# One block for both products of each MLP, and one two-column product for the sums of squares behind them

## The chip, the cores and the metric

One Trainium2 chip, one of its cores. The metric is device time in microseconds (us) of one execution of the whole kernel. The kernel before takes 2442.57 us, the median of three runs (2442.16 to 2447.31).

## The reference

The kernel computes two transformer layers and a third with a mixer and experts, for 512 tokens of 1024 features, in 32-bit floats. The change touches the MLP of the first two layers and the norm behind each:

```python
D_MODEL, SEQ, D_FF, NORM_EPS = 1024, 512, 4096, 1e-6

def rms_norm(x, g):
    xf = x.astype(jnp.float32)
    y = xf * lax.rsqrt(jnp.mean(xf * xf, axis=-1, keepdims=True) + NORM_EPS)
    return (y * g.astype(jnp.float32)).astype(x.dtype)

def modulate(h, shift, scale):
    return h * (1 + scale) + shift

def squared_relu_mlp(h, w1, w2):
    return jnp.square(jax.nn.relu(h @ w1)) @ w2

# in each of the first two layers
h = modulate(rms_norm(x, mlp_norm[layer]), sh_m, sc_m)
x = x + gt_m * squared_relu_mlp(h, mlp_w1[layer], mlp_w2[layer])
# behind the second layer: the final norm, and then the norm of the mixer of what it gives
x = rms_norm(x, final_norm)
```

Behind the first MLP one norm of x follows. Behind the second two norms follow each other (`final_norm`, then the mixer's), so two sums are needed for each token: of x squared, and of (x times the gain of `final_norm`) squared.

## The kernel before

Features lie on the partitions and tokens along the rows. `xT` is the residual stream (8 tiles of 128 features by 512 tokens), `hT` the normed input, `hid` (in `big`) the 32 tiles of hidden features, `ring` four slots of 2 MB for weights from memory. Every phase is a `Phase` with its own semaphores and a `Block`, in which each engine gets its instructions in the order written; at the end of a block all engines meet at a barrier, and GpSimd then clears the phase's semaphores one by one. No scheduler is at work: a semaphore wait in the text is a wait on the engine.

`phase_mlp` (line 862) is called twice, for "mlp1_a"/"mlp2_a" (here MLP A) and "mlp1_b"/"mlp2_b" (MLP B, with `inner`, the gain of `final_norm`). In both it holds two phases:

- Block 1, h @ w1. After a first chunk done plainly (L954) come 14 `pairs` with Winograd's form of Strassen's method: seven products `P1` to `P7` (L940) instead of eight, whose inputs are sums made on VectorE (L1037 to L1043) and whose results VectorE adds up (L1066 to L1083). ScalarE copies `P1` (L1019) and applies relu and square (L1002, L1004). Between these VectorE multiplies weights of the next conditioning vector (L890, `ada`), and adds their bias at the end (L1088).
- Block 2, hid @ w2. 32 `steps` in two halves of output features; each step has the seven products of two matmuls (L1148), with sums made by VectorE in `sums` (L1236 to L1251) one step ahead and one L890 per step. `outputs` (L1272 to L1292, `joined` L1258) adds a half into `xT`. ScalarE squares tiles of `xT` (L379; with the gain, L381). VectorE adds the squares of the first half's four tiles together (L390). TensorE sums squares over the features in `token_sums` (L1177): each of the four 128-token parts of a tile is loaded as weights and multiplied by a column of ones.

The tail of block 2 sets the end of the phase. On TensorE it is: `token_sums` of the accumulated first half (once for `sq1`, in MLP B again for `sq2`), four `keep_busy` products (L416) whose result nobody reads, `token_sums` of tiles j = 4 to 7 (in MLP B twice each), three `keep_busy`, and `spread_rows` (L407) with the inverse root. The buffers of squares alternate, so ScalarE waits for `token_sums` of j = 4 before it squares j = 6, and of j = 5 before j = 7. In MLP B VectorE makes the last two of the `sq2` squares (L1318).

```python
                for j in range(4, 8):
                    pe.wait_ge(sqd, j + 1)
                    token_sums(m.ps[:, 1, 0:NT], sq1.at(j), False, j == 7).then_inc(summed, 1)
                    if inner is not None:
                        pe.wait_ge(sqd2, j + 1)
                        token_sums(m.ps[:, 2, 0:NT], sq2.at(j), False, j == 7).then_inc(summed2, 1)
```

`prefetch` issues the loads of both streams from the sync engine's queue, each when its ring slot is free; weight chunks are released by TensorE, conditioning chunks by VectorE, in turn. In the experts, later, weights are loaded as fast as the memory gives them. The line numbers in the rows are those of the kernel before.

Of the kernel before, what the change touches and what calls it, by code (L numbers as in the profile page):

```python
# [21 lines left out]
ACT = mybir.ActivationFunctionType  # L22
# [839 lines left out]
def phase_mlp(nc, m, name1, name2, shift, gate, cvec, mod_out, mod_bias, width, gains, inner=None):  # L862
# [48 lines left out]

    with Phase(nc) as ph:
# [5 lines left out]
            "c22", "flat"))  # L918
        outs = [(shift, m.hT)]
        with nc.Block(no_gpsimd_drain=True) as block:  # L920
# [10 lines left out]
            @block.sync  # L931
            def _(sp):
                prefetch(m, sp, name1)

# [62 lines left out]

            @block.scalar
            def _(act):
                def squared(f, h, n):  # L1000
                    part = hid[:, f, h * H:(h + 1) * H]
                    act.activation(part, part, ACT.Relu).then_inc(flat, 1)  # L1002
                    act.wait_ge(flat, n)
                    act.activation(part, part, ACT.Square)  # L1004
# [4 lines left out]
                for j in range(4):  # L1009
                    act.wait_ge(mm, j + 1)  # L1010
                    act.activation(hid[:, j, :], m.ps[:, j, :], ACT.Relu).then_inc(relu, 1)  # L1011
                    act.wait_ge(relu, j + 1)
                    act.activation(hid[:, j, :], hid[:, j, :], ACT.Square)
                for i, (c, q) in enumerate(pairs):
# [12 lines left out]
                    squared(f, 1, 4 * i + 4)  # L1027

            @block.vector
            def _(dve):  # L1030
# [29 lines left out]
                for i, (c, q) in enumerate(pairs):  # L1060
# [29 lines left out]
    at2, n2 = STREAM[name2]  # L1090
    sq1, sq2 = Squares(m, 0), Squares(m, 3)
    steps = [(half, c, k) for half in range(2) for c in range(4) for k in range(4)]
    order = [4 * half + j for half in range(2) for j in (2, 3, 0, 1)]
    flat_h = m.hT[:].rearrange("p k t -> p (k t)")
    v1, v2, v3, v4 = oflat[:, 3072:3584], oflat[:, 3584:4096], flat_h[:, 3072:3584], flat_h[:, 3584:4096]
    cres = m.rs[:]
    inner2 = m.tmp[:, 1024:1032]

    def chunk2(half, c):
        return (at2 + 2 * (4 * half + c)) % RING, 16 * ((at2 + 2 * (4 * half + c)) // RING + 1)  # L1100

    def weight_quarters(half, c, k):
        w = m.ring[:, chunk2(half, c)[0], :].rearrange("p (k n) -> p k n", k=8)
        return w[:, k, 0:256], w[:, 4 + k, 0:256], w[:, k, 256:512], w[:, 4 + k, 256:512]

    def row_quarters(c, k):
        return hid[:, 8 * c + k, 0:H], hid[:, 8 * c + k, H:T], hid[:, 8 * c + 4 + k, 0:H], hid[:, 8 * c + 4 + k, H:T]

    def sums_of(s):
        return [oflat[:, 1536 * (s % 2) + 256 * j:1536 * (s % 2) + 256 * (j + 1)] for j in range(6)]  # L1110

    with Phase(nc) as ph:
        sem = ph.sem
        added, mod_done, chn, sqd, freed, sqd2, freed2, summed, whole, rooted, inverse = (
            sem(s) for s in ("added", "mod_done", "chn", "sqd", "freed", "sqd2",
                             "freed2", "summed", "whole", "rooted", "inverse"))
        summed2 = sem("summed2")
        prod, st12_ok, st3_ok, st4_ok, p1_ok, u2_ok, u4_ok, u3_ok, c22_ok, c11_ok, c21_ok, c12_ok, scaled = (
            sem(s) for s in ("prod", "st12_ok", "st3_ok", "st4_ok", "p1_ok", "u2_ok", "u4_ok", "u3_ok", "c22_ok", "c11_ok",
                             "c21_ok", "c12_ok", "scaled"))  # L1120
        with nc.Block(no_gpsimd_drain=True) as block:
            @block.sync
            def _(sp):
                prefetch(m, sp, name2)

            @block.tensor
            def _(pe):
                def products(s, names):
                    half, c, k = steps[s]
                    first, final = c == 0 and k == 0, c == 3 and k == 3  # L1130
                    a11, a12, a21, a22 = weight_quarters(half, c, k)
                    b11, b12, b21, b22 = row_quarters(c, k)
                    s1, s2, s4, t1, t2, t4 = sums_of(s)
                    of = dict(P1=(a11, b11), P2=(a12, b21), P3=(s4, b22), P4=(a22, t4), P5=(s1, t1), P6=(s2, t2), P7=(a21, b12))
                    for name in names:
                        if name == "P6":
                            pe.wait_ge(st12_ok, s + 1)
                        if name == "P7":
                            pe.wait_ge(st3_ok, s + 1)
                        if name == "P4":  # L1140
                            pe.wait_ge(st4_ok, s + 1)
                        if first and half:
                            for taken in dict(P1=[p1_ok], P6=[u2_ok], P5=[u4_ok, c22_ok], P7=[u3_ok], P2=[c11_ok], P4=[c21_ok],
                                              P3=[c12_ok])[name]:
                                pe.wait_ge(taken, 1)
                        a, b = of[name]
                        for q in range(2):
                            ins = pe.matmul(m.ps[:, bank[name], q * H:(q + 1) * H], a[:, q * P:(q + 1) * P], b,  # L1148
                                            start=(first and q == 0), stop=(final and q == 1))
                        ins.then_inc(prod, 1)  # L1150

                def released(chunk):


                    pe.wait_ge(prod, PRODUCTS * 4 * (chunk + 1))
                    pe.sem_inc(m.free[chunk2(chunk // 4, chunk % 4)[0]], 1)

                pe.wait_ge(m.full[chunk2(0, 0)[0]], chunk2(0, 0)[1])
                for s in (0, 1):
                    products(s, ["P1", "P2"])  # L1160
                for s in (0, 1):
                    products(s, ["P6", "P5", "P7", "P4", "P3"])
                for s in range(2, len(steps) - 2):
                    half, c, k = steps[s]
                    if k == 0:
                        pe.wait_ge(m.full[chunk2(half, c)[0]], chunk2(half, c)[1])
                    products(s, ["P1"])
                    if k == 0:
                        released(s // 4 - 1)
                    products(s, ["P6", "P5", "P7", "P2", "P4", "P3"])  # L1170
                for name in ("P1", "P6", "P5", "P7", "P2", "P4", "P3"):
                    for s in (len(steps) - 2, len(steps) - 1):
                        products(s, [name])

                def token_sums(out, sq, start, stop):
                    for i in range(NT):
# [24 lines left out]
            def _(act):  # L1201
                for half in range(2):
                    act.wait_ge(prod, PRODUCTS * 30 + 2 if half else PRODUCTS * 15 + 1)
                    if half:
                        act.wait_ge(c21_ok, 1)
# [2263 lines left out]
```

## Time and profile before

| what | value |
| --- | --- |
| median of 3 runs | 2442.57 us |
| the profiled execution, its own time | 2444.82 us |
| its span (first to last instruction) | 2443.0 us |
| TensorE busy | 2305.6 us, 94% |
| VectorE busy | 1125.5 us, 46% |
| ScalarE busy | 504.7 us, 21% |
| GpSimd busy | 43.0 us, 2% |
| mean of memory traffic | 189 GB/s |

Busy time is a share of the whole span, over stages with different limits; what a part of the kernel is worth is read from the timeline at its place. An instruction of TensorE in the program shows as two in the records of these 32-bit products (x16 is eight instructions). Idle time before a group stands in brackets with what ended it; "PEq" and a line is the sequencer of TensorE at that line, at the end of a block the barrier.

### The profile page before, as it was taken

How to read it: one execution, taken by the hardware profiler on the slowest of the kernel's cores; microseconds unless marked ns; L12 is line 12 of the kernel's file. 1: busy time of each engine (PE TensorE's matmuls, PEld its weight loads, DVE VectorE, ACT ScalarE, POOL GpSimd, SP SyncE). 2: the span in 40 equal slices, each digit the busy share in tenths (PEclk: the TensorE clock that was granted, in tenths of full speed). 3: DMA queues.
4: the chain of work that ended last, by engine and by line, in shares of the span. 5: the costliest groups of instructions: out<-in, count | busy, mean ns of one | idle time of the engine just before them, and what ended most of it. 6: DMA issues, size and time to landing. Idle time of an engine off the chain costs nothing. (4 is left out here: it accounts for less than half of the span.)

```text
span 2443.0 us, 25463 instructions
## 1 busy us (share of the span) xinstructions
PE 2305.6 (94%) x9476; PEld 1461.8 (60%) x9476; DVE 1125.5 (46%) x2602; ACT 504.7 (21%) x1140; POOL 43.0 (2%) x50
## 2 busy tenths in 40 slices
PE   7999899999999999989999999999999998889886
PEld 4444457888887655554688888854555443333332
DVE  4444435666776256661455667667524211111004
ACT  2233212330002144440333100112223000000001
POOL 0000000000000000000000000000000000000000
PEclk8999999999999899989999999999999999999999
DMA  7544213353532211102453435311032679999995
GB/s 302 219 175 165 103 69 138 143 202 138 206 139 112 62 59 52 61 35 103 175 204 144 201 142 203 138 69 69 1 138 104 253 309 427 427 426 426 423 424 223
DMA packets 45453, 452.65 MB, mean 185 GB/s; under 512 B 7784, under 2 KB 7784, under 8 KB 20240
## 3 DMA queue, kind: packets, MB, share of 16 engines
q1 hardware_dynamic: 37616, 435.64, 44.7%
q0 software_dynamic: 6528, 12.17, 1.4%
q10 hardware_dynamic: 1184, 3.19, 0.3%
q8 instruction: 77, 1.26, 0.2%
q14 instruction: 48, 0.39, 0.0%
HBM read 444.54 MB, written 18.39 MB: 189 GB/s over the span
## 5 line engine op out<-in xcount | busy, mean ns | idle before, releaser
L2857 PE MATMUL ps<-ring,big 128*64 128x512 f32 (+1 forms) x768 | 232.2, 609 | 27.9 <-issue 15.7
L1148 PE MATMUL ps<-big,ring 128*128 128x256 f32 x768 | 187.4, 382 | 4.4 <-PEq L920 4.4
L2857 PEld LDWEIGHTS ps<-ring,big 128*64 128x64 f32 (+1 forms) x768 | 85.0, 150 | 146.0 <-issue 132.8
L1148 PEld LDWEIGHTS ps<-big,ring 128*128 128x128 f32 x768 | 146.9, 192 | 25.4 <-issue 5.2
L537 PE MATMUL ps<-hT,ring 128*128 128x512 f32 x336 | 153.6, 607 | 5.6 <-DMA ring<-in_stream 5.6
L940 PE MATMUL ps<-hT,ring 128*128 128x256 f32 x672 | 154.3, 379 | 1.5 <-ACT big L1011 1.5
L2953 DVE TENSOR_TENSOR big<-big,ps 128x512 f32<-128x512 f32 x20 | 13.7, 687 | 294.4 <-ACT big L2922 280.3
L1938 PE MATMUL ps<-hT,ring 128*128 128x512 f32 x320 | 143.9, 605 | 2.7 <-DVE big L2320 1.7
L940 PEld LDWEIGHTS ps<-hT,ring 128*128 128x128 f32 x672 | 127.5, 190 | 20.3 <-issue 3.1
L890 DVE SCALAR_TENSOR_TENSOR ring<-ring,tmp 128x1024 f32<-128x1024 f32 x112 | 135.9, 1217 | 0.0
L2857 PE MATMUL ps<-big 128*64 128x512 f32 (+1 forms) x352 | 128.9, 600 | 7.1 <-ACT big L2918 3.3
L1148 PE MATMUL ps<-oT 128*128 128x256 f32 x512 | 120.8, 379 | 2.1 <-DVE oT L1247 2.1
L537 PEld LDWEIGHTS ps<-hT,ring 128*128 128x128 f32 x336 | 62.4, 192 | 84.2 <-issue 76.9
L814 PE MATMUL ps<-oT,ring 128*128 128x512 f32 x256 | 110.8, 593 | 1.4 <-PEq L1508 1.0
L1148 PEld LDWEIGHTS ps<-oT 128*128 128x128 f32 x512 | 97.1, 190 | 16.0 <-DVE oT L1247 2.9
L1938 PEld LDWEIGHTS ps<-hT,ring 128*128 128x128 f32 x320 | 60.8, 194 | 76.3 <-issue 74.4
L940 PE MATMUL ps<-oT 128*128 128x256 f32 x448 | 101.3, 379 | 0.0
L2857 PE MATMUL ps<-oT,big 128*64 128x512 f32 (+1 forms) x192 | 88.1, 614 | 7.7 <-issue 3.9
L2857 PE MATMUL ps<-hT,big 128*64 128x512 f32 (+1 forms) x192 | 88.2, 614 | 6.7 <-issue 3.7
L940 PEld LDWEIGHTS ps<-oT 128*128 128x128 f32 x448 | 85.1, 190 | 11.6
L1002 ACT ACTIVATE big<-big 128x256 f32<-128x256 f32 x112 | 46.7, 417 | 219.4 <-DVE big L1073 159.8
L814 PEld LDWEIGHTS ps<-oT,ring 128*128 128x128 f32 x256 | 48.3, 190 | 64.0 <-issue 64.0
(486 smaller groups left out, 3416.0 us busy)
## 6 DMA issues: line engine op xcount, KB each, us to landing
ring<-in_stream SPq DMA_DIRECT2D x99, 2048.0 KB, 8.5
ring<-in_gate SPq DMA_DIRECT2D x17, 2048.0 KB, 29.7
ring<-in_up SPq DMA_DIRECT2D x16, 2048.0 KB, 25.8
ring<-in_down SPq DMA_DIRECT2D x15, 2048.0 KB, 28.6
big<-in_up SPq DMA_DIRECT2D x9, 2048.0 KB, 25.1
big<-in_down SPq DMA_DIRECT2D x8, 2048.0 KB, 27.8
big<-in_gate SPq DMA_DIRECT2D x7, 2048.0 KB, 25.9
hT<-in_down SPq DMA_DIRECT2D x5, 2048.0 KB, 26.9
```

Of the source, the lines that this page charges most:

```text
L537: last = pe.matmul(m.ps[:, 2 + j, :], w[:, k, j * P:(j + 1) * P], m.hT[:, k, :], start=(k == 0), stop=(k == KT - 1))
L814: last = pe.matmul(m.ps[:, 4 * c + j, :], w[:, k, j * P:(j + 1) * P], actT[:, k, :], start=(k == 0), stop=(k == KT - 1))
L890: dve.scalar_tensor_tensor(w, w, 1.0, crow, ALU.mult, ALU.mult, accum_out=mod_out[:, o + j:o + j + 1]).then_inc(done, 1)
L940: ins = pe.matmul(out, a[:, k, :], b[:, k, :], start=(k == 0), stop=(k == 3))
L1002: act.activation(part, part, ACT.Relu).then_inc(flat, 1)
L1148: ins = pe.matmul(m.ps[:, bank[name], q * H:(q + 1) * H], a[:, q * P:(q + 1) * P], b, start=(first and q == 0), stop=(final and q == 1))
L1938: last = pe.matmul(m.ps[:, tile_bank(n), :], w[:, k, j * P:(j + 1) * P], m.hT[:, k, :], start=(k == 0), stop=(k == KT - 1))
L2857: ins = pe.matmul(out[a:z, :], left[:, k * P + a:k * P + z], bufs[i % WBUF][:, k * width + c * 512:k * width + (c + 1) * 512], start=(k == ...
L2953: dve.tensor_tensor(hid[:, s, :], hid[:, s, :], m.ps[:, 3 + 2 * s, :], ALU.mult).then_inc(hid_ok, 1)
```

## The change

In both MLPs the two phases become one: their semaphores are all taken at the start, `prefetch(m, sp, name2)` stands behind `prefetch(m, sp, name1)` on the sync engine, and each engine's instructions of block 2 follow those of block 1 without a barrier. What the barrier had held apart is now held by semaphores (`prod`, `p1_ok`, `c11` and the like at 14, `squared_ok` for the hidden tiles). The last `ada` of block 1 goes behind the first `sums` of block 2, and both bias additions become one at the end. The sums of squares go to PSUM bank 7 as pairs of columns; the moving operand has two columns. The accumulated first half is summed within step 24 of 32. In MLP B the second column carries the factor gain squared, so j = 4 to 7 need no scaled squares of their own. VectorE prepares these factors behind block 1.

```diff
             def _(sp):
                 prefetch(m, sp, name1)
+                prefetch(m, sp, name2)
...
+                def token_sums(sq, factor, start, stop):
+                    for i in range(NT):
+                        ins = pe.matmul(m.ps[:, 7, 2 * i:2 * i + 2], sq[:, i * P:(i + 1) * P], factor,
+                                        start=(start and i == 0), stop=(stop and i == NT - 1))
+                    return ins
...
+                        if first and not half:
+                            for taken in dict(P1=[p1_ok], P6=[u2_ok], P5=[u4_ok, c22], P7=[u3_ok], P2=[c11], P4=[c21],
+                                              P3=[c12])[name]:
+                                pe.wait_ge(taken, len(pairs))
...
                 pe.wait_ge(m.full[chunk2(0, 0)[0]], chunk2(0, 0)[1])
+                pe.wait_ge(squared_ok, squares_of(0))
...
                     products(s, ["P6", "P5", "P7", "P2", "P4", "P3"])
+                    if s == 24:
+                        pe.wait_ge(freed, 3)
+                        if inner is None:
+                            token_sums(sq1.acc, m.ones[:, 0:2], True, False)
+                        else:
+                            pe.wait_ge(freed2, 3)
+                            pe.wait_ge(weighed, 1)
+                            token_sums(sq1.acc, either[:, 0, :], True, False)
+                            token_sums(sq2.acc, either[:, 1, :], False, False)
...
-                pe.wait_ge(u4_ok, 2)
-                pe.wait_ge(freed, 3)
-                token_sums(m.ps[:, 1, 0:NT], sq1.acc, True, False)
-                if inner is not None:
-                    pe.wait_ge(c22_ok, 2)
-                    pe.wait_ge(freed2, 3)
-                    token_sums(m.ps[:, 2, 0:NT], sq2.acc, True, False)
                 released(7)
-                keep_busy(m, pe, 7, 4)
+                pe.wait_ge(v1_ok, 2)
+                keep_busy(m, pe, 0, 4)
                 for j in range(4, 8):
                     pe.wait_ge(sqd, j + 1)
-                    token_sums(m.ps[:, 1, 0:NT], sq1.at(j), False, j == 7).then_inc(summed, 1)
-                    if inner is not None:
-                        pe.wait_ge(sqd2, j + 1)
-                        token_sums(m.ps[:, 2, 0:NT], sq2.at(j), False, j == 7).then_inc(summed2, 1)
-                keep_busy(m, pe, 7, 3)
+                    token_sums(sq1.at(j), m.ones[:, 0:2] if inner is None else factors[:, order[j], :], False, j == 7
+                               ).then_inc(summed, 1)
+                keep_busy(m, pe, 0, 3)
...
-                        if inner is not None and j < 6:
+                        if inner is not None and j < 4:
                             square_rows(m, act, sq2, inner, j, freed2, sqd2, order[j])
...
                     if i + 1 < len(pairs):
                         sums_b(*pairs[i + 1], i + 1)
-                    ada(c, 2 * q + 1, 2 * q + 2)
-                dve.wait_ge(mod_done, 8 * tiles)
-                dve.tensor_tensor(mod_out[:, 0:8 * tiles], mod_out[:, 0:8 * tiles], mod_bias[:, 0:8 * tiles], ALU.add)
+                        ada(c, 2 * q + 1, 2 * q + 2)
...
                 if inner is not None:
-                    c1.link(dve.tensor_tensor(inner2, inner, inner, ALU.mult))
+                    dve.wait_ge(c11, len(pairs))
+                    c2.link(dve.memset(factors[:, :, 0], 1.0))
+                    c2.link(dve.memset(either, 0.0))
+                    for j in range(2):
+                        c2.link(dve.memset(either[:, j, j:j + 1], 1.0))
+                    dve.tensor_tensor(factors[:, :, 1], inner, inner, ALU.mult).then_inc(weighed, 1)
                 sums(0)
+                ada(7, 3, 4)
...
                 outputs(1)
-                if inner is not None:
-                    for j in (6, 7):
-                        f = order[j]
-                        dve.wait_ge(summed2, j - 5)
-                        dve.scalar_tensor_tensor(sq2.at(j), m.xT[:, f, :], inner2[:, f:f + 1], m.xT[:, f, :], ALU.mult, ALU.mult
-                                                 ).then_inc(sqd2, 1)
```

Where the blocks of MLP A meet, on VectorE: first the rows before (L1083 is the last addition of block 1, L1088 the bias addition, L1236 to L1251 are `sums(0)`), then those of the change.

```order
L1083 TENSOR_TENSOR big<-tmp,ps 128x256 [waits u4_ok,prod]
L890 SCALAR_TENSOR_TENSOR ring,mod<-ring,tmp 128x1024
L1088 TENSOR_TENSOR mod<-mod,vec 128x32 [waits mod_done]
L920 UNCONDITIONAL_BRANCH
L1223 UNCONDITIONAL_BRANCH [waits barrier_Pool_Activation_PE_DVE_SP_release]
L1236 TENSOR_TENSOR oT<-ring 128x256 [waits full2]
L1237 TENSOR_TENSOR oT<-oT,ring 128x256 [waits chn]
L1240 TENSOR_TENSOR oT<-big 128x256
L1241 TENSOR_TENSOR oT<-big,oT 128x256 [waits chn]
```

```order
L1223 TENSOR_TENSOR big<-tmp,ps 128x256 [waits u4_ok,prod]
L1242 TENSOR_TENSOR oT<-ring 128x256 [waits prod,squared_ok,full2]
L1243 TENSOR_TENSOR oT<-oT,ring 128x256 [waits chn2]
L1246 TENSOR_TENSOR oT<-big 128x256
L1247 TENSOR_TENSOR oT<-big,oT 128x256 [waits chn2]
L1248 TENSOR_TENSOR ring<-ring 128x256
L1250 TENSOR_TENSOR big<-big 128x256
L1256 TENSOR_TENSOR oT<-ring,oT 128x256 [waits st12_ok]
L1257 TENSOR_TENSOR oT<-big,oT 128x256 [waits chn2]
L890 SCALAR_TENSOR_TENSOR ring,mod<-ring,tmp 128x1024
```

The barrier and the bias addition are gone from between the blocks, the first sums follow the last addition directly, and the L890 stands behind them.

The tail of MLP B on TensorE, before and then with the change (L1177 and L1040 are `token_sums`, L416 `keep_busy`, L407 `spread_rows`):

```order
L1148 MATMUL ps<-big,oT 128x256 x4
L1177 MATMUL ps<-ones,hT 128x1 x8
L416 MATMUL ps<-con 128x128 x4
L1177 MATMUL ps<-ones,hT 128x1 x32
L416 MATMUL ps<-con 128x128 x3
L407 MATMUL ps<-con,st 128x128 x4
```

```order
L1068 MATMUL ps<-big,oT 128x256 x4
L416 MATMUL ps<-con 128x128 x4
L1040 MATMUL ps<-tmp,hT 128x2 x16
L416 MATMUL ps<-con 128x128 x3
L407 MATMUL ps<-con,st 128x128 x4
```

Of 40 instructions of `token_sums` 16 are left in the tail, and 8 stand in step 24; in MLP A 16 of 20 are left and 4 stand in step 24.

## Rows read from the trace of the kernel before

**Rows 1.** The page, 40 slices of the span: TensorE's clock and DMA, in tenths
```profile
PEclk8999999999999899989999999999999999999999
DMA  7544213353532211102453435311032679999995
```

**Rows 2.** Timeline, MLP A from block 1 to block 2: start us, us, engine, line
```profile
556.88 1.89 PE L940 MATMUL ps<-hT,rs 128*128 128x256 f32 x8
...
559.15 1.22 DVE L890 SCALAR_TENSOR_TENSOR ring<-ring,tmp 128x1024 f32<-128x1024 f32 x1
...
561.50 5.30 PE L1148 MATMUL ps<-big,ring 128*128 128x256 f32 x16 [2.72 <-PEq L920]
561.50 0.42 DVE L1236 TENSOR_TENSOR oT<-ring 128x256 f32<-128x256 f32 x1 [0.78 <-PEq L920]
...
564.56 0.42 DVE L1236 TENSOR_TENSOR oT<-ring 128x256 f32<-128x256 f32 x1
...
566.64 1.89 PE L1148 MATMUL ps<-oT 128*128 128x256 f32 x8
```

**Rows 3.** Busy time by stretch, the same place: the clock stands behind POOL's column
```profile
562.00:563.00 1.00, 1.00 (x4) 0.77 (x3) 0.97 (x3) 0.00 (x0) 0.00 (x0) 0.50 0.99 426
```

**Rows 4.** Timeline, MLP B from block 1 to block 2
```profile
1363.25 1.89 PE L940 MATMUL ps<-hT,rs 128*128 128x256 f32 x8
...
1365.51 0.18 DVE L1088 TENSOR_TENSOR mod<-mod,vec 128x24 f32<-128x24 f32 x1
...
1366.84 3.69 PE L1148 MATMUL ps<-big,ring 128*128 128x256 f32 x16 [1.70 <-PEq L920]
1366.84 0.17 DVE L1302 TENSOR_TENSOR tmp<-vec 128x8 f32<-128x8 f32 x1 [1.15 <-PEq L920]
1367.04 0.42 DVE L1236 TENSOR_TENSOR oT<-ring 128x256 f32<-128x256 f32 x1
...
1368.30 0.42 DVE L1241 TENSOR_TENSOR oT<-big,oT 128x256 f32<-128x256 f32 x1
...
1370.37 1.89 PE L1148 MATMUL ps<-oT 128*128 128x256 f32 x8
```

**Rows 5.** Timeline, the tail of MLP A
```profile
759.37 0.95 PE L1177 MATMUL ps<-ones,hT 128*128 128x1 f32 x8
...
759.69 1.26 ACT L379 ACTIVATE hT<-xT 128x512 f32<-128x512 f32 x2 [9.88 <-DVEq L1263]
...
760.18 1.14 PE L416 MATMUL ps<-con 128*128 128x128 f32 x8
...
761.16 5.38 PE L1177 MATMUL ps<-ones,hT 128*128 128x1 f32 x32
761.21 1.12 DVE L1258 SCALAR_TENSOR_TENSOR xT<-rs,mod,xT 128x256 f32<-128x256 f32 x2
```

**Rows 6.** Timeline, the tail of MLP B
```profile
1561.98 1.84 PE L1177 MATMUL ps<-ones,hT 128*128 128x1 f32 x16
...
1563.69 1.14 PE L416 MATMUL ps<-con 128*128 128x128 f32 x8
...
1564.66 10.35 PE L1177 MATMUL ps<-ones,hT 128*128 128x1 f32 x64
```

**Rows 7.** Busy time by stretch, where the clock falls in the two tails
```profile
762.00:763.00 1.00, 1.00 (x10) 1.00 (x10) 0.76 (x4) 0.63 (x1) 0.00 (x0) 0.87 0.80 344
...
1568.00:1569.00 1.00, 1.00 (x8) 1.00 (x7) 0.67 (x1) 0.12 (x1) 0.00 (x0) 0.64 0.99 426
```

**Rows 8.** Timeline behind the tail of MLP A: TensorE and GpSimd in the next phase
```profile
770.13 1.80 PE L416 MATMUL ps<-con 128*128 128x128 f32 x14 [0.42 <-PEq L1121]
...
771.86 0.53 POOL L1371 MEMSET big<- 128x512 f32 x1 [771.40 <-issue]
```

**Rows 9.** Busy time by stretch, an unbroken stretch of MLP B's block 1
```profile
1175.00:1363.00 188.00, 187.27 (x822) 155.90 (x821) 101.72 (x201) 54.68 (x129) 0.00 (x0) 1.00 0.42 167
```

More of the change, by code:

```diff
@@ L996, in _, with products @@
                 pe.sem_inc(m.free[chunk1(7)[0]], 1)
+                def token_sums(sq, factor, start, stop):
[3 more added lines that the diff above has]
+                    return ins
+                def products(s, names):
+                    half, c, k = steps[s]
+                    first, final = c == 0 and k == 0, c == 3 and k == 3
+                    a11, a12, a21, a22 = weight_quarters(half, c, k)
+                    b11, b12, b21, b22 = row_quarters(c, k)
+                    s1, s2, s4, t1, t2, t4 = sums_of(s)
+                    of = dict(P1=(a11, b11), P2=(a12, b21), P3=(s4, b22), P4=(a22, t4), P5=(s1, t1), P6=(s2, t2), P7=(a21, b12))
+                    for name in names:
+                        if name == "P6":
+                            pe.wait_ge(st12_ok, s + 1)
+                        if name == "P7":
+                            pe.wait_ge(st3_ok, s + 1)
+                        if name == "P4":
+                            pe.wait_ge(st4_ok, s + 1)
+                        if first and not half:
+                            for taken in dict(P1=[p1_ok], P6=[u2_ok], P5=[u4_ok, c22], P7=[u3_ok], P2=[c11], P4=[c21],
+                                              P3=[c12])[name]:
+                                pe.wait_ge(taken, len(pairs))
+                        if first and half:
+                            for taken in dict(P1=[v1_ok], P6=[v2_ok], P5=[v4_ok, c22_ok], P7=[v3_ok], P2=[c11_ok], P4=[c21_ok],
+                                              P3=[c12_ok])[name]:
+                                pe.wait_ge(taken, 1)
+                        a, b = of[name]
+                        for q in range(2):
+                            ins = pe.matmul(m.ps[:, bank[name], q * H:(q + 1) * H], a[:, q * P:(q + 1) * P], b,
+                                            start=(first and q == 0), stop=(final and q == 1))
+                        ins.then_inc(prod2, 1)
@@ new lines, in released @@
+                def released(chunk):
+                    pe.wait_ge(prod2, PRODUCTS * 4 * (chunk + 1))
+                    pe.sem_inc(m.free[chunk2(chunk // 4, chunk % 4)[0]], 1)
+                pe.wait_ge(m.full[chunk2(0, 0)[0]], chunk2(0, 0)[1])
+                pe.wait_ge(squared_ok, squares_of(0))
+                for s in (0, 1):
+                    products(s, ["P1", "P2"])
+                for s in (0, 1):
+                    products(s, ["P6", "P5", "P7", "P4", "P3"])
+                for s in range(2, len(steps) - 2):
+                    half, c, k = steps[s]
+                    if k == 0:
+                        pe.wait_ge(m.full[chunk2(half, c)[0]], chunk2(half, c)[1])
+                        pe.wait_ge(squared_ok, squares_of(c))
+                    products(s, ["P1"])
+                    if k == 0:
+                        released(s // 4 - 1)
+                    products(s, ["P6", "P5", "P7", "P2", "P4", "P3"])
+                    if s == 24:
[7 more added lines that the diff above has]
+                            token_sums(sq2.acc, either[:, 1, :], False, False)
@@ new lines, in _ @@
+                for name in ("P1", "P6", "P5", "P7", "P2", "P4", "P3"):
+                    for s in (len(steps) - 2, len(steps) - 1):
+                        products(s, [name])
+                released(7)
+                pe.wait_ge(v1_ok, 2)
+                keep_busy(m, pe, 0, 4)
+                for j in range(4, 8):
+                    pe.wait_ge(sqd, j + 1)
+                    token_sums(sq1.at(j), m.ones[:, 0:2] if inner is None else factors[:, order[j], :], False, j == 7
+                               ).then_inc(summed, 1)
```

233 lines of the change are left out of this document (90 added, 143 removed).

## The prediction

> **What bounds the kernel now.** I read the slices of the page first: in the slices from about a sixth to three quarters of the span DMA is far from full while TensorE's clock stands at nine tenths or more; only the experts at the end show DMA full [rows 1]. Their weights are loaded behind a routing that needs everything before it, so whatever the MLPs save, or lose, moves the rest as a block and reaches the end one for one. Inside the MLPs TensorE is the bound: in a long stretch it is busy 187.27 of 188 us [rows 9]. So the questions are where TensorE stands or crawls at the places that the change touches. The timeline shows four: two seams between block 1 and block 2, and two tails.
>
> Seam A: the last product group of block 1 starts at 556.88, TensorE then stands 2.72 us for the barrier and starts block 2 at 561.50. The first 16 records of block 2 take until 566.64, 5.14 us [rows 2]; at seam B the same 16 take 1366.84 to 1370.37, 3.53 us [rows 4]. The reason is the clock: behind the pause of seam A it is granted at 0.50, 1.2 instead of 2.4 GHz [rows 3]; behind the 1.70 us of seam B nothing slows.
>
> Tails: here TensorE is busy, but with `token_sums`. 16 records take 1561.98 to 1563.69 at the full clock, 0.107 us each [rows 6]. During them the clock falls, at about 762.7 in tail A and 1568.3 in tail B [rows 7], 3.4 and 6.3 us behind the last real product, and from there a record takes about 0.215 us (30 records in the last 6.6 us of tail B). From the last product to the end of the sums tail A takes 759.37 to 766.54, 7.2 us, and tail B 1561.98 to 1575.01, 13.0 us, since it has 80 records of sums against 40 [rows 5, 6]. The squares are ready earlier: in tail A VectorE's last two additions end at 762.33 [rows 5].
>
> **The change, part by part.** The sum is made against the profiled execution's own 2444.82 us.
>
> *Seam A.* Before: spacing of records is 0.216 us (eight in 1.89 with a last one of 0.38), so block 1 issues its last until 556.88 + 8 x 0.216 = 558.6, and step 0 reaches `P6` at 566.64: 8.0 us [rows 2]. With the change TensorE waits for its own last product before it releases the chunk. Such a drain without a barrier is not in these rows; its lower bound is nothing, its upper one the 0.16 us by which a record outlasts the spacing plus the 0.42 us that a whole barrier takes behind an engine that ends last [rows 8]. I take 0.45 us, near the upper end, since some six semaphore waits follow. Then 3.5 us for the 16 records at full clock: 3.95. Gain 8.0 - 3.95 = 4.1 us, of which 1.6 is clock.
>
> What is late next there is VectorE, which must have `sums(0)` ready for `P6`. Its first free moment is 559.15 [rows 2]; from the first sum to the fourth it takes 1367.04 to 1368.72, 1.7 us [rows 4]: ready at 560.9, needed at 558.6 + 3.95 = 562.5. The `ada` now stands before `sums(1)`: 559.15 + 3.06 (one round of sums, 561.50 to 564.56) + 1.3 for L890 + 1.7 = 565.2, needed 20 records later at 566.8. Covered by 1.6 us both times; were the cover gone, the price is that delay, once. The `ada` also frees its ring slot some 3 us later, and the sync queue's next weights chunk stands behind that load; but a slot is wanted again only after four steps of 28 records, 4 x 28 x 0.216 = 24 us, so 3 us are hidden.
>
> *Seam B.* Before: 1363.25 + 1.73 = 1365.0 to 1370.37, 5.4 us; after 3.95. Gain 1.4 us. VectorE has five small chained operations ahead of `sums(0)`, at 0.20 us each (L1302 to the next start [rows 4]): 1365.5 + 1.0 + 1.7 = 1368.2, needed at 1368.95. Covered by 0.7; bounds of the uncovered cost 0 and, if the tiny memsets take twice that, 0.3. I take 0.
>
> *Sums in step 24.* 8 records in MLP A and 16 in MLP B now stand in the unbroken stream: 0.86 + 1.71 us, and 0.1 each for the entry: 2.7 us lost. They aren't covered by anything, since TensorE is the bound; in exchange they leave the tails, which is counted there. The bounds are 0.107 us a record and, with a low clock behind them, what the rival below gives.
>
> *Tails.* The new tails are alike: drain 0.45, four `keep_busy` 0.97 (1563.69 to 1564.66 [rows 6]), then four groups of 8 records. The first two start at 1.4 and 2.3 us behind the last product; the squares for them are there (the first two end at 759.69 + 1.26 = 760.95 in tail A, 1.6 us behind it [rows 5]). The third waits for its square: VectorE's first addition of the last pair ends at 1.84 + 0.56 = 2.4, the square takes 0.63, so 3.2; the fourth by the same path 4.0. At full clock that ends at 5.1. With the clock falling after 3.4 us, as in tail A, groups take 1.72 instead of 0.86, and the end is at 6.6; with a fall after 6.3 us, as in tail B, it is at 5.1 still. Nothing tells the two apart beforehand, so I take the middle, 5.9. Gain: tail A 7.2 - 5.9 = 1.3 us; tail B 13.0 - 5.9 = 7.1 us.
>
> That a second column is free rests on this: eight `keep_busy` records with 128 columns take 0.97 us, 0.121 each, and one-column records 0.107 [rows 6]. 127 columns more cost 0.014 us, so what is paid is the load of the 128x128 weights. The Trainium skill, "TensorE: Matmul & The Clock Gate", section "Back-to-back issue gap", gives for an isolated product of 1 to 64 columns a floor of about 25 ns. By that, an estimate from the page, 32 records fewer would save only 0.8 us in tail B; the row says four times as much for each record, and the row decides.
>
> *The rest.* One bias addition and some squares less on VectorE and ScalarE are beside TensorE: 0. GpSimd clears twice as many semaphores behind the merged block. Now its first work comes at 771.86, 1.7 us behind TensorE's at 770.13 [rows 8], so others don't wait for the clearing: 0, upper bound another 1.7 us for each MLP.
>
> **Sum:** 4.1 + 1.4 - 2.7 + 1.3 + 7.1 = 11.2 us, so 2433.6 for an execution like the profiled one. The median of the runs is 2.25 us below that execution, and part of that may be seam A's 1.6 us of clock. If the runs of the median have that loss, 2442.57 - 11.2 = 2431.4; if not, 2442.57 - 9.6 = 2433.0. I say **2432.2**. The Trainium skill, same page, section "What's actually happening", says that the number of slow products differs from run to run of one kernel; by it seam A's fall is a matter of the run, and the second figure is the better.
>
> **Rivals.**
> - *Tails cold from the start.* The clock could fall as soon as a tail begins: 1.4 + 4 x 1.72 + 0.1 = 8.4 us each, 2.5 more each: 2437.2. For it: long runs of these records did bring the clock down [rows 7]. Against: never within the first 3.4 us. Chance 0.10.
> - *Tails warm throughout.* 5.1 each, and the eight records of `spread_rows` at full clock, 8 x (0.215 - 0.121) = 0.8 each: 3.2 us more gained, 2429.0. For it: tail B kept the clock for 6.3 us. Chance 0.09.
> - *The sums of step 24 pull the clock down.* 16 records are 1.7 us; a pause of 1.70 did not [rows 4], one of 2.72 did [rows 2]. Price 1.6 us each, 2435.4. Chance 0.06.
> - *Columns are paid.* Then the change does not do what it says: a two-column record costs as two of one column, tail B loses its gain of 32 records x 0.16 = 5.1 us, tail A pays 5.1 more and step 24 24 x 0.107 = 2.6: 2445.0. Against: the row of `keep_busy`. Chance 0.04.
> - *Slower: the long unbroken stream lowers the clock.* The merged block runs TensorE without a pause for some 370 us in each MLP. Should the chip grant less behind, say, 200 us, each per cent of the remaining 170 us costs 1.7 us; two MLPs at a clock lower by 3.3% eat the 11.2 us, and at a clock lower by a tenth the time is 2432.2 + 34 = 2466. Against: 1.00 over 188 us, and in MLP B only 1.70 us of pause between two such stretches [rows 4, 9]. The Trainium skill, same page, section "Seeing it yourself", tells of a current limiter that acts from a third busy core of a die on; this kernel has one, and no run here shows it. Chance 0.03.
>
> **How the numbers follow.** The forecast, from 2430.5 to 2435, has 0.68. A measurement here can tell about 0.2% from no change, 4.9 us, so 2437.7 is the border. Faster: 0.68 + 0.09 + 0.06 and half of the first rival, 0.88. Within: the other half and the columns, 0.09. Slower 0.03. The range takes in the warm and the cold tails, with some tenths for the drain and the small operations: 2429.0 to 2437.8.
>
> **What would show it.** At both seams TensorE restarts about 0.45 us after its last product, with no record of 0.50 clock behind; `P6` of step 0 comes some 4 us behind the last product, without a wait for VectorE. In step 24, 8 and 16 records at 0.107 us. In the tails the sums end 5 to 6.6 us behind the last product in both MLPs. I am wrong if `P6` waits for VectorE at seam B, if the two-column records are spaced much wider than 0.107 us at full clock, if step 24 is followed by a low clock, or if the experts' part changes its length.

## The result

On the chip of the first comparison the change takes **2427.98 us** (median of 5 runs, 2426.54 to 2430.14) against 2442.57 us (5 runs, 2439.78 to 2447.45): ratio 0.9936, 95% interval 0.9921 to 0.9951, 14.6 us less. On the chip of the first eight experiments the same two kernels stand at 2426.72 and 2446.05 us, ratio 0.992 (0.9907 to 0.9934), 19.3 us less. Forecast were 2432.2 us and 10.4 us less; the time is 1.0 us below the low end of the range. The time fell on the side that had the chance of 0.88, but the gain was forecast too small.

**The seams.** The profiled execution of the change has 2426.54 us, span 2424.8. Its timeline at seam A (start us, us, engine, line), to be held against [rows 2]:

```profile
558.71 1.89 PE L978 MATMUL ps<-hT,rs 128*128 128x256 f32 x8
...
560.91 3.69 PE L1068 MATMUL ps<-big,ring 128*128 128x256 f32 x16 [0.30 <-PE ps L978]
560.98 0.42 DVE L1242 TENSOR_TENSOR oT<-ring 128x256 f32<-128x256 f32 x1
...
562.23 0.42 DVE L1247 TENSOR_TENSOR oT<-big,oT 128x256 f32<-128x256 f32 x1
...
564.43 0.81 PE L1068 MATMUL ps<-oT 128*128 128x256 f32 x3
```

TensorE is idle for 0.30 us in place of 2.72; the 16 records take 561 to 564.4 at 0.22 us each instead of 0.32. From the start of the last group to `P6` it is 5.72 us, where [rows 2] have 9.76: 4.04 less. VectorE's fourth sum ends at 562.65, 1.8 us before `P6` wants it. In the busy time by stretch, the clock column (behind POOL's) has no 0.50 left, against [rows 3]:

```profile
562.00:563.00 1.00, 1.00 (x7) 0.87 (x6) 0.97 (x4) 0.00 (x0) 0.00 (x0) 1.00 0.37 66
```

The timeline of seam B, against [rows 4]:

```profile
1354.63 1.89 PE L978 MATMUL ps<-hT,rs 128*128 128x256 f32 x8
...
1356.82 3.69 PE L1068 MATMUL ps<-big,ring 128*128 128x256 f32 x16 [0.30 <-PE ps L978]
1356.93 0.07 DVE L1309 MEMSET tmp<- 128x8 f32 x1
...
1357.53 0.43 DVE L1242 TENSOR_TENSOR oT<-ring 128x256 f32<-128x256 f32 x1
...
1358.78 0.42 DVE L1247 TENSOR_TENSOR oT<-big,oT 128x256 f32<-128x256 f32 x1
...
1360.35 1.03 PE L1068 MATMUL ps<-oT 128*128 128x256 f32 x4
```

Again 5.72 us, where there were 7.12: 1.40 less. The five small operations of VectorE take 0.6 us together, and its sums are ready at 1359.20, 1.15 us early.

**Step 24 and the tails.** The timeline of step 24 in MLP B: sixteen two-column records stand 1.70 us apart from first to next, as sixteen one-column records did in [rows 6].

```profile
1509.36 1.84 PE L1040 MATMUL ps<-tmp,hT 128*128 128x2 f32 x16
1511.06 1.11 PE L1068 MATMUL ps<-big,ring 128*128 128x256 f32 x4
```

The tails in the timeline, MLP A and MLP B, against [rows 5, 6], and GpSimd's first work behind tail B:

```profile
756.36 1.89 PE L1068 MATMUL ps<-big,oT 128*128 128x256 f32 x8
...
758.40 1.13 PE L416 MATMUL ps<-con 128*128 128x128 f32 x8
...
759.37 5.27 PE L1040 MATMUL ps<-ones,hT 128*128 128x2 f32 x32
...
1551.72 1.89 PE L1068 MATMUL ps<-big,oT 128*128 128x256 f32 x8
...
1554.73 5.32 PE L1040 MATMUL ps<-tmp,hT 128*128 128x2 f32 x32
...
1563.66 1.13 PE L407 MATMUL ps<-con,st 128*128 128x128 f32 x8 [0.41 <-PEq L957]
...
1567.38 0.12 POOL L1920 MEMSET big<- 128x24 f32 x1 [406.93 <-issue]
```

The last product is issued until 756.36 + 8 x 0.216 = 758.09, and the sums end at 764.64, 6.55 us later; in tail B 6.60. GpSimd is free only 3.7 us after TensorE's restart at 1563.66, and nothing waits for it. The clock falls some 3.3 us behind the last product in both tails, by the busy time per stretch (compare [rows 7]):

```profile
761.00:762.00 1.00, 1.00 (x7) 0.95 (x7) 0.50 (x4) 0.75 (x2) 0.00 (x0) 0.67 0.82 344
762.00:763.00 1.00, 1.00 (x6) 1.00 (x6) 0.00 (x0) 0.00 (x0) 0.00 (x0) 0.50 1.15 492
...
1556.00:1557.00 1.00, 1.00 (x9) 0.95 (x8) 0.74 (x3) 0.82 (x2) 0.00 (x0) 0.82 0.98 377
```

**Where the rest came from.** The places of the sum give 10.1 us in this pair of profiles (table below). The spans differ by 18.2. Most of what is missing lies in stages that the change doesn't touch. The compression (`phase_cmp`) and the nsa stage (`phase_nsa`) follow MLP A, the mix stage (`phase_mix`) follows MLP B. The first two, by stretch from one's first product to the next's, first in the kernel before, then in the change (stretch, length, busy time of PE, PEld, DVE, ACT, POOL, clock, DMA share, GB/s):

```profile
771.77:830.64 58.87, 56.24 (x280) 40.36 (x279) 24.62 (x61) 18.49 (x30) 1.67 (x3) 0.91 0.09 27
830.64:1103.88 273.24, 260.98 (x1200) 144.13 (x1201) 153.75 (x512) 118.84 (x341) 0.00 (x0) 0.96 0.17 56
```

```profile
769.88:827.14 57.26, 54.62 (x280) 38.74 (x279) 24.63 (x61) 18.48 (x30) 1.66 (x3) 0.94 0.09 28
827.14:1096.35 269.21, 256.84 (x1200) 142.11 (x1201) 153.78 (x512) 118.83 (x341) 0.00 (x0) 0.98 0.18 56
```

The same records, but 332.1 us against 326.5: 5.6 us, with TensorE's clock at 0.91 and 0.96 against 0.94 and 0.98.

### The profile page after: what moved, and what is told of

Its sections match the earlier page's. It is cut to its first block and busy times, and to the rows that moved or that the text cites. A ratio compares the mean times of both kernels' runs of the same rounds, so it can differ in the third digit from the quotient of the medians.

```text
span 2424.8 us, 25390 instructions
## 1 busy us (share of the span) xinstructions
PE 2291.9 (95%) x9444; PEld 1449.6 (60%) x9444; DVE 1124.4 (46%) x2602; ACT 503.4 (21%) x1138; POOL 42.9 (2%) x50
## 5 line engine op out<-in xcount | busy, mean ns | idle before, releaser
L2864 PE MATMUL ps<-ring,big 128*64 128x512 f32 (+1 forms) x768 | 232.7, 610 | 27.7 <-issue 15.9
L2960 DVE TENSOR_TENSOR big<-big,ps 128x512 f32<-128x512 f32 x20 | 13.8, 688 | 293.8 <-ACT big L2929 279.7
L890 DVE SCALAR_TENSOR_TENSOR ring<-ring,tmp 128x1024 f32<-128x1024 f32 x112 | 136.1, 1219 | 0.0
```

Of the source, the lines that this page charges most:

```text
L890: dve.scalar_tensor_tensor(w, w, 1.0, crow, ALU.mult, ALU.mult, accum_out=mod_out[:, o + j:o + j + 1]).then_inc(done, 1)
L2864: ins = pe.matmul(out[a:z, :], left[:, k * P + a:k * P + z], bufs[i % WBUF][:, k * width + c * 512:k * width + (c + 1) * 512], start=(k == ...
L2960: dve.tensor_tensor(hid[:, s, :], hid[:, s, :], m.ps[:, 3 + 2 * s, :], ALU.mult).then_inc(hid_ok, 1)
```

## The experiments

e1 to e8 ran on one chip, e9 to e12 on another. The kernel before has a median of 2446.05 us beside the first four, 2445.89 beside the next four and 2445.86 beside the last four, on the other chip (15, 21 and 21 runs), so times of the two are held together here.

**e1_before_again**: the kernel before, unchanged.

> The kernel before, unchanged, with a second profile. In the first profiles the change gained 10.1 us inside the two MLPs but 18.2 us of span; 6.7 us of the rest lie between the MLPs (from the first product behind MLP A to the last product group of MLP B's block 1: 593.1 us before, 586.4 after) and 3.2 us behind MLP B, where nothing was changed. Theory chance: where TensorE's clock falls in those stretches differs from execution to execution; then this profile gives the same instructions another length between the MLPs, anywhere from 584 to 596 us, with other places of half clock, and the time is the same as before within 0.2%. Rival systematic: the change itself speeds up what lies outside; then this profile shows 592 to 594 us between the MLPs again.

Measured: 2445.75 us (2442.01 to 2447.69, 11 runs), ratio 0.9999 (0.999 to 1.0008). Its profile shows what one profile of before had hidden. The tail of MLP B in its timeline:

```profile
1560.15 1.84 PE L1177 MATMUL ps<-ones,hT 128*128 128x1 f32 x16
1561.85 1.14 PE L416 MATMUL ps<-con 128*128 128x128 f32 x8
1562.83 13.19 PE L1177 MATMUL ps<-ones,hT 128*128 128x1 f32 x64
```

From 1560.15 to 1576.02 it is 15.9 us, where [rows 6] gave 13.0: the clock fell earlier. At seam A the low clock is there again (0.50 from 564 on). The nsa stage takes 270.73 us instead of 273.24, and from the first product behind MLP A to the start of the last group of MLP B's block 1 it is 587.9 us instead of 591.5. So the same kernel has other lengths in untouched stages from one execution to the next, as the theory of chance said, though the medians of the two kernels stay 19.3 us apart.

**e2_after_again**: the change, unchanged.

> The changed kernel with a second profile. Theory chance: its stretch between the MLPs varies too, 584 to 596 us, and the median is 2428 within 2 us. Rival systematic: 586 to 587 us again.

Measured: 2426.72 us (2425.33 to 2428.14, 5 runs), ratio 0.992 (0.9907 to 0.9934). Both tails keep the full clock here; in the timeline the 32 records take 3.76 us in place of 5.27 and 5.32:

```profile
761.16 3.76 PE L1040 MATMUL ps<-ones,hT 128*128 128x2 f32 x32
...
1556.57 3.76 PE L1040 MATMUL ps<-tmp,hT 128*128 128x2 f32 x32
```

The sums end 5.0 us behind the last product, the forecast's figure for the full clock (5.1). The stretch between the MLPs takes 586.4 us, where the first profile of the change had 584.8: in this second pair the two kernels are 1.4 us apart in it, in the first they were 6.7. With this second pair the sum can be held against two executions of each kernel:

| place | forecast gain | first pair | second pair | mean |
|---|---|---|---|---|
| seam A | 4.1 | 4.0 | 4.1 | 4.1 |
| seam B | 1.4 | 1.4 | 1.4 | 1.4 |
| step 24, by the length of block 2, both MLPs | -2.7 | -2.4 | -2.4 | -2.4 |
| tail A | 1.3 | 0.6 | 2.1 | 1.3 |
| tail B | 7.1 | 6.4 | 10.8 | 8.6 |
| sum of the places | 11.2 | 10.1 | 16.0 | 13.0 |
| everything else | 0 | 8.1 | 2.5 | 5.3 |
| span | 11.2 | 18.2 | 18.5 | 18.4 |

**e3_seam_only** and **e4_sums_only**: the two halves of the change. e3 merges the blocks and leaves every sum where and as it was:

```
                     products(s, ["P6", "P5", "P7", "P2", "P4", "P3"])
-                    if s == 24:
...
+                pe.wait_ge(freed, 3)
+                token_sums(m.ps[:, 1, 0:NT], sq1.acc, True, False)
+                if inner is not None:
+                    pe.wait_ge(freed2, 3)
+                    token_sums(m.ps[:, 2, 0:NT], sq2.acc, True, False)
                 released(7)
```

> The merged block, but with the sums of squares as before (one column, both sets, all in the tail). My prediction: seams give 4.1 + 1.4 us in a profile like the first, 3.9 to 5.5 with or without the clock's fall at seam A; so 2437.1 to 2438.7, and the tails 7.2 and 13.0 us as before. If something outside the seams gains from the merging (rival systematic), more than 7 us.

e4 keeps both blocks and the barrier, and takes over the two-column sums with those of step 24:

```
+                    if s == 24:
+                        pe.wait_ge(freed, 3)
+                        if inner is None:
+                            token_sums(sq1.acc, m.ones[:, 0:2], True, False)
+                        else:
...
-                    token_sums(m.ps[:, 1, 0:NT], sq1.at(j), False, j == 7).then_inc(summed, 1)
...
+                    token_sums(sq1.at(j), m.ones[:, 0:2] if inner is None else factors[:, order[j], :], False, j == 7
```

> The two phases with the barrier kept, but the two-column sums and step 24. My prediction: 7.1 + 1.3 - 2.7 = 5.7 us, so 2436.9; from the first profile of the change (tails 8.9 to 8.3 and 14.8 to 8.3 us from the last product group, step 24 costing 0.9 and 1.5 us) 4.6 us, so 2438.0. If e3 and e4 add up to the 14.6 us of the whole change they share them as 5 + 5 and the rest is with one of them; if they add up to 10, the rest is chance in the medians of before.

Measured: e3 2435.66 us (2434.1 to 2437.57), ratio 0.9957 (0.9943 to 0.9971), 10.4 less; e4 2435.33 us (2434.21 to 2437.99), ratio 0.996 (0.9946 to 0.9974), 10.7 less. At their places both do what the sum says; e3's timeline has the 0.30 us seam, e4's the short tail:

```profile
561.56 3.69 PE L1064 MATMUL ps<-big,ring 128*128 128x256 f32 x16 [0.30 <-PE ps L976]
```

```profile
1559.13 1.89 PE L1156 MATMUL ps<-big,oT 128*128 128x256 f32 x8
...
1562.14 4.45 PE L1132 MATMUL ps<-tmp,hT 128*128 128x2 f32 x32
```

But their parts of the sum are 5.5 us (4.1 + 1.4) and 5.7 us (1.3 + 7.1 - 2.7), some 5 us less than the medians show for each; both stand about 1.5 us below the low end expected of them. e3 is past the 7 us that its expectation had set as the mark of a gain outside the seams, and the two halves add up to 21.1 us, against 19.3 for the whole change on the same chip. The MLPs together are 4.0 us (e3) and 7.7 us (e4) shorter than the mean of before's two profiles, the rest of the program 4.2 and 2.8 us. The compression takes 57.2 us instead of 58.9 in both, the nsa stage 269.5 instead of 270.7 to 273.2 in e3.

**Dead work as a probe.** "Dead" products are `keep_busy` products, whose result nobody reads; "arrival" is the moment at which a stage is reached. If unchanged stages change their length with the moment at which they are reached, work that does nothing must be able to make the kernel faster. Into the kernel before, behind step 24:

```
+                    if s == 24 and inner is None:
+                        keep_busy(m, pe, 7, 4)
```

> The kernel before with four more products that nobody reads (eight records, 0.97 us of full-clock work) in step 24 of MLP A, where TensorE is the bound. Theory additive: whatever is put there costs its length: 2446.05 + 1.0 = 2447.0. Theory arrival (the unchanged stages behind lose more or less of TensorE's clock according to when they are reached): behind MLP A the phases cmp and nsa took 332.1 and 329.6 us in both profiles of before, with 30.7 and 23.9 us at half clock, and 326.5 to 326.8 us in those of the change and of the seam alone, with 17.0. Being 1 us later should bring nsa to a better place: 2 to 3 us less there, so 2444 to 2446, faster than before though work was added.

> As e5, with eleven products (22 records, 2.7 us). Additive: 2448.7. Arrival: cmp 57.2 instead of 58.9 us and nsa 269.5 instead of 271 to 273: 2.7 - 1.6 - 2.5 = -1.4, so 2444.6, range 2443.5 to 2446.

> The kernel before with eight dead products (16 records of 0.121 us, 1.9 us) behind step 24 of MLP A. If time is added one for one: 2445.9 + 1.9 = 2447.8. If the stages behind MLP A cost less or more of TensorE's clock by when they are reached, as four (2438.4) and eleven dead products (2443.9) suggest: between these two, 2439 to 2444, with 57.2 us for the compression and about 269.6 us for the nsa stage, 326.8 together, where the kernel before has 329.6 to 332.1.

e10 has `inner is not None` there: the same products in MLP B.

> The kernel before with four dead products (1.0 us) behind step 24 of MLP B, not of MLP A: the control to the run in which the same products in MLP A made the kernel 7.5 us faster. If that gain came through the stages behind MLP A (arrival), it is gone here: these two stages keep the 329.6 to 332.1 us of the kernel before, and the time is 2446.9, give or take 3 us for the stages behind MLP B, whose arrival does shift. If the dead products help by themselves, wherever they stand, the time is about 2438.4 again.

And the same line (4, 8 or 11) in step 24 of the change:

> The changed kernel with the same four products (0.97 us) in step 24 of MLP A. Additive: 2427.3 + 1.0 = 2428.3. Arrival: cmp goes back to 58.9 us and nsa to 272 to 273: 1.0 + 1.6 + 3.3 = +5.9, so 2433, range 2430.5 to 2434.

> The change with eight dead products (1.9 us) in step 24 of MLP A. One for one: 2427.4 (between the two medians of the change, 2426.7 and 2428.0) + 1.9 = 2429.3. Arrival: 2429 to 2434, the two stages behind MLP A together between 326.6 (the good place) and 332.1 us (the bad one).

> The change with eleven dead products (2.7 us) in step 24 of MLP A. One for one: 2430.1. Arrival: it now reaches the stages behind MLP A nearly when the kernel before does, so they should take 329.6 to 332.1 us together in place of 326.6, and the time should be 2427.4 + 2.7 + 3 to 5.5 = 2433 to 2435.6. With the runs of 0, 4 and 8 products on either kernel, less the products' own time, this gives the worth of the change as a mean over four arrivals: 11.2 us if my sum of the parts was right and only the arrival was missing from it, 14 and more if the parts themselves were undersized.

The timeline of e5 shows what the four products cost by themselves: 8 records in 0.90 us; the 22 records of eleven take 2.46.

```profile
719.78 1.05 PE L416 MATMUL ps<-con 128*128 128x128 f32 x8
720.68 1.03 PE L1148 MATMUL ps<-big,ring 128*128 128x256 f32 x4
```

| run | median (range, runs) | ratio (95%) | compression + nsa, us | mix, us |
|---|---|---|---|---|
| before, two profiles | 2445.9 | | 332.1, 329.6 | 228.0, 224.5 |
| e5: before, 4 | 2438.40 (2436.07 to 2441.99, 10) | 0.9973 (0.9964, 0.9983) | 326.8 | 225.4 |
| e9: before, 8 | 2443.52 (2442.52 to 2446.04, 10) | 0.9995 (0.9986, 1.0005) | 332.1 | 224.6 |
| e6: before, 11 | 2443.87 (2441.09 to 2446.55, 11) | 0.9997 (0.9988, 1.0005) | 326.8 | 225.4 |
| e10: before, 4 in MLP B | 2440.12 (2436.6 to 2444.61, 10) | 0.9978 (0.9968, 0.9987) | 329.6 | 222.0 |
| change, two profiles | 2428.0, 2426.7 | | 326.5, 326.8 | 224.6, 226.9 |
| e7: change, 4 | 2431.67 (2427.7 to 2437.39, 6) | 0.9949 (0.9933, 0.9964) | 330.2 | 227.3 |
| e11: change, 8 | 2428.57 (2427.02 to 2431.86, 4) | 0.9933 (0.9914, 0.9952) | 330.3 | 223.8 |
| e12: change, 11 | 2434.29 (2431.98 to 2438.84, 6) | 0.9958 (0.9946, 0.9971) | 330.3 | 223.8 |

Four dead products make the kernel before 7.5 us **faster**. That is the sign that arrival asked for, but 5.6 us below the low end of its range (2444), so the size was not foreseen. In its profile the two stages are those of the change; the same two stretches in e5:

```profile
773.58:830.80 57.22, 54.59 (x281) 38.71 (x279) 24.21 (x60) 18.05 (x30) 1.32 (x3) 0.94 0.09 28
830.80:1100.40 269.60, 257.20 (x1201) 142.07 (x1201) 153.71 (x512) 118.72 (x341) 0.00 (x0) 0.98 0.17 56
```

In the change the same four products cost 4.3 us by the mean of its two medians (2427.4), as expected of e7 (2430.5 to 2434), though its interval of 0.9933 to 0.9964 and the change's two (0.9907 to 0.9934, 0.9921 to 0.9951) touch; the nsa stage of e7 has before's length:

```profile
827.39:1100.33 272.94, 260.59 (x1201) 144.21 (x1201) 153.71 (x512) 118.90 (x341) 0.00 (x0) 0.96 0.17 56
```

The control e10 came out half as expected. With the products behind these two stages, the stages keep before's 329.6 us, as arrival says; but the time fell by 5.7 us, 3.8 below the low end of 2443.9 (2446.9 - 3), and in its profile the mix stage behind MLP B is the shorter one. Its three stretches (compression, nsa, mix):

```profile
774.34:833.22 58.88, 56.25 (x281) 40.37 (x279) 24.61 (x61) 18.50 (x30) 1.67 (x3) 0.91 0.09 27
833.22:1103.96 270.74, 258.38 (x1201) 142.69 (x1201) 153.75 (x512) 118.76 (x341) 0.00 (x0) 0.97 0.17 56
1581.73:1803.70 221.97, 216.40 (x883) 123.04 (x881) 144.28 (x277) 60.25 (x119) 0.00 (x0) 0.98 0.13 48
```

By its time alone e10 is nearer to "the products help by themselves". What speaks against that is where the gain stands: not in the MLPs, which take 829.2 us together in e5 and 831.1 in e10 (before 828.3 and 831.6), but in stages behind them, in e5 in those behind MLP A and in e10 in the one behind MLP B. So a gain by arrival can come up in any later stage, and the stages behind MLP A are only one place. Nor could I tell which: e9's two stages were expected at 326.8 us and took 332.1, though its time lay in the range; e11's took 330.3, and its median of 2428.57 lies 0.7 us from simple addition (2429.3) and below the range of arrival (from 2429); e7's compression kept 57.2 us. e12 met both its stages (330.3) and its time (2433 to 2435.6). e6's time lay in its range, but its profile is the fastest of its eleven runs, so its stages say little of its median.

What the traces show is narrower than arrival. The length of a stage goes with the place in it at which the clock falls. In the nsa stage the granted clock falls to half late in the stage in all 14 profiles. Where the first of these low stretches begins 227.7 to 228.4 us behind the stage's first product, the stage takes 269.2 to 269.6 us (the change, e2, e3, e5, e6, e8); where it begins at 228.6 to 229.1, 272.9 to 273.2 us, with twice as much time at half clock (before, e4, e7, e9, e11, e12); at 229.2, 270.7 us (e1, e10). In the compression it begins at 31.8 to 32.1 us in the four profiles with 58.9 us, and at 32.4 to 33.4 in the ten with 57.2. So two tenths of a microsecond in the place (228.35 us in e5, 228.56 in e7) go with 3.3 us in the length. But the moment counted from the start of the program doesn't tell the place. e9 reaches the compression at 773.56 us, e5 at 773.58, and they have different lengths; e9's:

```profile
773.56:832.44 58.88, 56.25 (x281) 40.37 (x279) 24.60 (x61) 18.49 (x30) 1.67 (x3) 0.91 0.09 27
```

And the 14 profiles reach MLP A, ahead of which nothing was changed, anywhere from 358.3 to 362.7 us, a wider spread than the 0.9 to 2.5 us of dead work. That dead work lowers the time is shown by ten runs of e5 and ten of e10; that it does so by moving these stages is the reading that fits best, but with one profile for each padded kernel it can't be told from the chance of that execution.

**What the change is worth by itself.** Less the dead products' own 0.9, 1.8 and 2.5 us, the four arrivals (0, 4, 8, 11) of before give 2445.9, 2437.5, 2441.7 and 2441.4, and of the change 2427.4, 2430.8, 2426.8 and 2431.8. The differences are 18.5, 6.7, 14.9 and 9.6 us, in the mean 12.4, with a standard error of 2.6. That agrees with the 13.0 us inside the MLPs, and does not part 11.2 from 14.6.

The profiles give a sharper figure, since they can be split. In the six profiles of the kernel before, with and without dead work (before, e1, e5, e6, e9, e10), the two MLPs take 829.0 us in the mean, less the dead products' own time; in the five of the change (after, e2, e7, e11, e12) 817.2. The difference is 11.9 us with a standard error of 0.9, against a forecast of 11.2. Everything outside the MLPs takes 1610.9 and 1609.5 us: 1.4 us apart, with a standard error of 1.6. So outside the MLPs no gain of the change itself can be told, and the 5.3 us of the two pairs come from the unpadded kernel before, whose two profiles have the longest rest of all 14 (1614.7 and 1613.2 us; the others 1606.4 to 1612.5).

**e8_after_tail_sums**: the change with the accumulated sums back in the tail.

```
-                    if s == 24:
-                        pe.wait_ge(freed, 3)
...
+                pe.wait_ge(freed, 3)
+                if inner is None:
+                    token_sums(sq1.acc, m.ones[:, 0:2], True, False)
+                else:
...
                 released(7)
```

> The changed kernel, but the accumulated first half is summed in the tail again (in two columns), not in step 24. My prediction priced the step at 0.107 us a record, 2.7 us lost in the stream and as much gained in the tails. By the timeline the tail can take them more cheaply: with work behind the last product the drain isn't waited for, 0.5 us less in each MLP: 1 us faster, 2426 to 2426.5. Rival: the clock falls earlier behind the last product, so that two groups more run at half clock: 1 to 3 us slower, up to 2430.

Measured: 2427.38 us (2422.52 to 2430.56, 6 runs), ratio 0.9927 (0.9912 to 0.9942). No difference to the change can be told; moving these sums to step 24 is neither a gain nor a loss that shows.

## Why the prediction was right and wrong

- **Seams: right.** 4.1 and 1.4 us forecast, 4.0 to 4.1 and 1.4 measured, in both pairs. The drain was put at 0.45 us behind the last issue; TensorE restarts 0.47 us behind it (558.71 + 1.73 = 560.44 to 560.91), of which 0.30 are idle. VectorE was covered by 1.8 and 1.15 us (forecast 1.6 and 0.7).
- **Two columns for the price of one: right.** 0.107 us a record at full clock. "Columns are paid" is out.
- **Step 24: right** within 0.3 us, with no low clock behind it; that rival is out too. Costs put at nothing (GpSimd's clearing, the bias addition) stayed there.
- **Tails: the mechanism right, tail B's size off.** 5.9 us behind the last product were forecast between 5.1 and 6.6; the first profile shows 6.6 twice, the second 5.0 twice. So "tails warm throughout" is no rival but what some executions do; "cold from the start" (8.4) was seen in neither. The mis-sized term is before's tail B, taken from one execution: 13.0 us there, 15.9 in e1, 15.6 in e3, 13.1 to 13.8 in e5, e6, e9 and e10. With the mean of the two pairs the term is 8.6 in place of 7.1; with all profiles of either kernel it is 8.5, and tail A's 0.9 in place of 1.3.
- **The slower rival: absent.** In the merged block of MLP B, 408.5 us, the clock stays at full until the tail (mean 0.99, as before).
- **The step that failed** is in the first paragraph of the prediction: "whatever the MLPs save, or lose, moves the rest as a block and reaches the end one for one". The rest isn't a block. The compression takes 57.2 or 58.9 us, the nsa stage 269.2 to 273.2, the mix stage 222.0 to 228.0, with the same products and another share of them at the half clock, and which of these an execution gets goes with the place in the stage at which the clock falls. The unpadded kernel before had poor places in both of its profiles: all four shifts tried on it came out lower, by 2.0 to 7.5 us with the dead work included, though two of them (e6, e9) by no more than the runs can tell. In the mean of the two pairs of profiles this gave 5.3 us on top of 13.0. Over all padded and unpadded profiles the sum of the parts was nearly right (11.9 us in the MLPs for 11.2 forecast): what the forecast lacked was the length of the untouched stages. It put their change at nothing from the order of the work alone, without a look at how their clock falls.
- **The correction for the median was wrong too.** I took 0.8 us off the gain (10.4 in place of 11.2), for a seam A that might be at full clock in the other runs. All seven profiles of kernels with the barrier (before, e1, e4, e5, e6, e9, e10) show the low clock there. The rule of the Trainium skill that I leaned on ("TensorE: Matmul & The Clock Gate", section "What's actually happening": the number of slow products differs from run to run) holds in this case, by the 270.7 and 273.2 us of the nsa stage in one kernel; at seam A it did not apply.
- **My own test failed.** I wrote that I am wrong "if the experts' part changes its length": it did not in the first pair (525.0 against 524.8 us), and I was off all the same; in the second pair it did (522.6 against 525.9). The test looked at the one stage that DMA bounds, and asked of a single pair what varies between executions.

What stays open: what sets the place at which the clock falls in a stage, why each shift lands where it does, and how e5 and e6 come to differ by 5.5 us in the median (their profiled executions are 1.2 us apart, but e6's is its fastest run). The difference of the two medians, 14.6 us on one chip and 19.3 on another, is larger than what the change is worth by itself, about 12 us: known to 0.9 us inside the MLPs by the profiles, and to 2.6 us as a whole by the medians.

## What to carry to other kernels

Sum a change's parts at their places, and then ask whether the unchanged stages behind it keep their length: in a program whose TensorE clock falls in many places, shifts of one to three microseconds moved the total by up to 7.5. Before a difference of that size is called an edit's, pad both kernels with a few amounts of dead work and compare the means, and in their profiles compare the changed stages and the untouched ones apart. Take every term in which the clock falls from at least two profiles.

## What the runs showed of the hardware

A second column in a product with 128x128 fp32 weights was free (0.107 us with one or with two). A wait of TensorE for its own last product cost 0.30 us of idle time, a barrier at the same place 1.70 to 2.72. A pause of 2.72 us was followed by the half clock, one of 1.70 us and the new 0.30 us weren't; and in the old tails the clock fell though TensorE was busy for the whole time, with products of one column behind it. An unchanged stage took 269.2 to 269.6 us or 272.9 to 273.2, according to whether the clock's first late fall came 227.7 to 228.4 us into it or 228.6 to 229.1. The unexpected one: 0.9 us of dead products took 7.5 us off the kernel before; on the change they put 4.3 us on, a difference that is less sure.
